# The weighted sum of gathered rows: from VectorE and TensorE half and half to TensorE alone

## What is computed

```python
def one(args):
    hh, ee, gg = args
    a = jnp.einsum("tkd,td->tk", peer_down[ee], hh, preferred_element_type=jnp.float32)
    act = (gg * jax.nn.gelu(a)).astype(hh.dtype)
    return jnp.einsum("tk,tkd->td", act, peer_up[ee])
```

## Time and profile before

| | us |
|---|---|
| median of 3 runs | 5476.44 |
| lowest, highest | 5467.74, 5490.61 |
| the profiled execution | 5502.99 |
| its span, first to last instruction | 5501.2 |
| TensorE matmuls busy, mean granted clock | 3615.6, 0.731 |
| VectorE busy | 2942.9 |
| GpSimd busy | 1960.8 |
| ScalarE busy | 816.3 |
| DMA moved | 1321.25 MB, of which 1073.87 by the indirect fetches |

### The profile page before, as it was taken

The page is one execution under the profiler, slowest core; times in us unless marked ns, Lnnn a source line. Parts: engine busy times, 40 slices in busy tenths (PEclk is TensorE's granted clock), DMA queues, the critical chain, the costliest instruction groups (busy, mean ns, idle before and its releaser), DMA issues.

```text
span 5501.2 us, 34464 instructions
## 1 busy us (share of the span) xinstructions
PE 3615.6 (66%) x9742; PEld 1773.4 (32%) x9742; DVE 2942.9 (53%) x5957; ACT 816.3 (15%) x1938; POOL 1960.8 (36%) x2058
## 2 busy tenths in 40 slices
PE   5778646887567667757575467751478885554566
PEld 1256413554212234315321111120256653221111
DVE  1211696547945766652476874540342223778766
ACT  1110112211101211111111110110131101111111
POOL 0000355435534656640254464430100000544665
PEclk8879757888688788865766567776688877666556
DMA  4235689988889999980487699870200003877999
GB/s 178 72 89 151 234 275 337 336 300 315 298 324 359 373 359 379 386 317 31 176 321 270 227 374 346 334 271 21 75 1 1 1 0 127 331 283 274 361 370 329
DMA packets 481787, 1321.25 MB, mean 240 GB/s; under 512 B 39884, under 2 KB 138444, under 8 KB 481088
## 3 DMA queue, kind: packets, MB, share of 16 engines
q0 software_dynamic: 294912, 1073.87, 52.4%
q1 hardware_dynamic: 179672, 219.30, 12.2%
q10 hardware_dynamic: 7016, 25.88, 1.3%
HBM read 1314.08 MB, written 1.17 MB: 239 GB/s over the span
## 4 chain that ended last, share of the span: by engine, by line
issue 22%; PE 20%; DMA 11%; POOL 8%; DVE 6%; SPq 2%; ACT 2%; another core or an unknown queue 1%; DVEq 0%; ACTq 0%; POOLq 0%
PE ps L1293 19%; POOL arena L2324 8%; DMA arena<-in_peer_up,arena 4%; DVE arena L637 2%; DMA arena<-in_peer_v,arena 2%; DVE arena L650 1%; DMA arena<-in_ada_w 1%; DMA arena<-in_peer_u,arena 1%; ACT arena L1878 1%; DVE ps L650 1%; SPq L2444 1%; DMA arena<-in_w_mod 1%; DMA arena<-mod_scratch 1%; PE ps L1299 1%
## 5 line engine op out<-in xcount | busy, mean ns | idle before, releaser
L1293 PE MATMUL ps<-arena 128*128 128x512 f32 (+12 forms) x9164 | 3501.1, 537 | 1555.9 <-DMA arena<-in_peer_up,arena 525.2
L1293 PEld LDWEIGHTS ps<-arena 128*128 128x128 f32 (+5 forms) x9164 | 1677.8, 216 | 3323.9 <-issue 2356.4
L650 DVE SCALAR_TENSOR_TENSOR arena<-arena,ps 128x1024 f32<-128x1024 f32 x1024 | 1245.2, 1216 | 394.2 <-DMA arena<-in_peer_down,arena 179.2
L2324 POOL DMA_INDIRECT arena<-in_peer_down,arena x768 | 723.4, 942 | 1715.1 <-DVE arena L654 965.9
L2324 POOL DMA_INDIRECT arena<-in_peer_up,arena x768 | 730.2, 951 | 476.7 <-issue 216.0
L650 DVE SCALAR_TENSOR_TENSOR ps<-arena,ps 128x512 f32<-128x512 f32 x1016 | 764.5, 753 | 190.9 <-DMA arena<-in_peer_up,arena 89.6
L1878 ACT ACTIVATE arena<-arena 128x128 f32<-128x128 f32 (+4 forms) x1251 | 448.3, 385 | 2586.2 <-issue 786.5
L2324 POOL DMA_INDIRECT arena<-in_peer_u,arena x256 | 240.5, 939 | 945.0 <-DVE arena L654 842.4
L637 DVE TENSOR_TENSOR arena<-ps,arena 128x512 f32<-128x512 f32 (+2 forms) x182 | 125.5, 690 | 636.5 <-PE ps L1293 598.9
L637 DVE TENSOR_TENSOR arena<-arena 128x16 f32<-128x16 f32 (+9 forms) x399 | 266.9, 669 | 222.4 <-DMA arena<-arena 148.1
L1878 ACT ACTIVATE arena<-ps 128x256 f32<-128x256 f32 (+3 forms) x341 | 172.9, 507 | 1274.8 <-PE ps L1293 896.8
(11 more groups left out here) (35 smaller groups left out, 563.4 us busy)
## 6 DMA issues: line engine op xcount, KB each, us to landing
arena<-in_w_mod SPq DMA_DIRECT2D x24, 2048.0 KB, 9.4
arena<-in_w_in SPq DMA_DIRECT2D x72, 512.0 KB, 5.5
arena<-in_w_pq SPq DMA_DIRECT2D x12, 2048.0 KB
arena<-in_ada_w SPq DMA_DIRECT2D x12, 2048.0 KB
arena<-in_w_in SPq DMA_DIRECT2D x8, 2048.0 KB, 20.0
arena<-in_w_out SPq DMA_DIRECT2D x8, 2048.0 KB, 7.7
arena<-mod_scratch ACTq DMA_DIRECT2D x30, 512.0 KB, 8.5
arena<-in_peer_down,arena POOLq DMA_INDIRECT x768
```

The source lines that it names most:

```text
L650: self.e.scalar_tensor_tensor(o, a, s, b, op0, op1, accum_out=accum).then_inc(*(inc or self.inc(self.S.vec)))
L1293: return self.e.matmul(o, l, r, start=start, stop=stop)
L2324: self.e.indirect_dma_start(out=o, out_offset=None, in_=table, in_offset=bass.IndirectOffsetOnAxis(ap=idx.bitcast(U32), axis=0)).then_inc( ...
```

## The change

For the up rows of a step TensorE makes two products with the same diagonal, columns 0 to 511 into `K.ap` and 512 to 1023 into `K.av`, and the second one increments `S.up_tensor`. VectorE's pass over the up rows, its waits for them and the semaphore `S.up_vector` are gone; POOL waits for `S.up_tensor` alone. In `fold`, `S.sum_read` is incremented by the third pass instead of the first.

```diff
@@ Vector.gather
                 n, k = divmod(u, NEXT)
                 c = base + u
-                w = K.AW[n % 2][:, k:k + 1]
-                self.wait_ge(S.up_in[c % NU], 16 * (c // NU + 1))
-                if k % GK == 0:
-                    self.wait_ge(*self.weighted)
-                src = K.us[c % NU][:, 512:1024]
-                if c:
-                    self.wait_ge(S.up_vector, c)
-                if k == 0:
-                    if c:
-                        self.wait_ge(S.tile_done, c // NEXT)
-                    self.ts(K.av, src, w, None, M, None, inc=self.inc(S.up_vector), free=True)
-                else:
-                    self.stt(K.av, src, w, K.av, M, AD, inc=self.inc(S.up_vector), free=True)
@@ Vector.fold
-        self.tt(K.tpb, K.ap, gr[:, 0:512], M, inc=self.inc(S.sum_read))
+        self.tt(K.tpb, K.ap, gr[:, 0:512], M)
         self.tt(self.X(t)[:, 0:512], self.X(t)[:, 0:512], K.tpb, AD)
-        self.tt(K.tpb, K.av, gr[:, 512:1024], M)
+        self.tt(K.tpb, K.av, gr[:, 512:1024], M, inc=self.inc(S.sum_read))
@@ Tensor.gather
-                self.mm(K.ap, K.dg[c % 4], K.us[c % NU][:, 0:512], k == 0, k == NEXT - 1).then_inc(*self.inc(S.up_tensor))
+                self.mm(K.ap, K.dg[c % 4], K.us[c % NU][:, 0:512], k == 0, k == NEXT - 1)
+                self.mm(K.av, K.dg[c % 4], K.us[c % NU][:, 512:1024], k == 0, k == NEXT - 1).then_inc(*self.inc(S.up_tensor))
@@ Pool.gather
                     self.wait_ge(S.up_tensor, c - NU + 1)
-                    self.wait_ge(S.up_vector, c - NU + 1)
```

More of the change, by code:

```diff
@@ L2591, in semaphores @@
     S.down_in, S.up_in = several("down_in", ND), several("up_in", NU)
-    S.diagonal, S.up_vector, S.up_tensor = one("diagonal"), one("up_vector"), one("up_tensor")
+    S.diagonal, S.up_tensor = one("diagonal"), one("up_tensor")
     S.sum_read, S.tile_done, S.keys_in = one("sum_read"), one("tile_done"), one("keys_in")
```

## The result

The changed kernel took 5503.95 us (median of ten runs, 5484.43 to 5520.59), the kernel before 5481.47 (ten, 5464.27 to 5509.59): ratio 1.0036, interval 1.0019 to 1.0053. Timed twice more, later, it gave 0.9997 (0.9978 to 1.0017) and 1.0002 (0.9980 to 1.0025). So the change costs between nothing and 0.4%, inside the half percent that I called no change. I had forecast 5550 and a slowdown as the likeliest case: the median moved by 22 us where I had 78.

What follows compares the result with a forecast made beforehand. Gather stretches alternate: clean ones paced by POOL's queue and DMA, others with VectorE or TensorE full. Terms -48 + 100 + 10 + 12 + 4 = +78 gave 5581 profiled, 5554 on the median, stated as 5550; range 5420 to 5680.

Steps and rivals of the forecast that it cites:

- Item 1: Gather stretches where VectorE is full, and phase starts: removing its passes saves 48 us, bounds -75 and -25.
- The two stretches: 620:820 and 1400:1540 us, VectorE full with top-k arithmetic woven in: 22 and 20 us gained.
- The step's cost: TensorE's time for a gather step with two products: 2.00 us at the full clock, 3.85 at the half one.
- Rival (c): Clean gather stretches: the clock is low for half of the 382 steps, +200 us on top, 5750; chance 0.08.
- The full stretch: 1040 to 1180 us, TensorE busy 134.7 of 140 us: the added products cost +25 us.
- rival (b): TensorE has room even where it looks full, so its woven stretches cost 0: sum -22, 5454; chance 0.08.
- item 2: Woven gather stretches with TensorE full or nearly: 0.90 us more a step, sum +100 us, bounds +50 and +150.
- 1560:1700: Woven stretch in us, 30 steps: 27 us of new work against 25 idle on TensorE, priced at +18.
- 3380:3520: Woven stretch in us, 23 steps: 21 us of new work against 25 idle, much before ada_w blocks; +15.
- 1800:2340: Woven stretch in us, 178 steps: TensorE 90% full beside a DMA share of 1.00; +20.
- Items 3 to 5: Costs in clean stretches (+10 us), at the ends of the phases (+12) and in the fold (+4).
- Rival (a): Woven stretches: TensorE's idle time takes the passes and VectorE's release had held the fetches; sum -32, 5444; chance 0.20.

Runs made afterwards that it cites:

- e2: Changed kernel without the second product, so nobody forms the upper half and the fold reads the lower half twice; 5308.74 us, ratio 0.9901 to the kernel before.
- e6: Changed kernel without the second product, but VectorE still waits in its queue for each up row; 5445.43 us against 5500.36, ratio 0.9898.
- e1: Kernel before with VectorE's pass kept and TensorE making the second product as well; 5423.97 us against 5360.32, ratio 1.0125.
- e3: Changed kernel in the first tile only (steps 0 to 127), the kernel before in the rest; 5352.59 us, ratio 0.9982.
- e7: Changed kernel with a third product a step in steps 256 to 511; 5597.15 us against 5500.36 of the kernel before, ratio 1.0172.
- e8: Changed kernel, but VectorE takes up steps 110 to 185 and from 256 on, its half sum copied at hand-over; 5458.42 us against 5488.45, ratio 0.9958.
- e11: e8 with VectorE's sum of up steps 110 to 185 kept in SBUF, without copy or wait; 5328.91 us against 5364.09 of the kernel before, ratio 0.9942.

## Why the forecast was wrong, step by step

**Item 1 was right in its sum.** -48 forecast; -53 (e2) and -56 (e6) measured. The two stretches hold less of it than I said, -17 and -17 us where I had -22 and -20; in e6's column the rest lies just around them, in the woven stretches and at the start of the second phase.

**The step's cost was right.** 503 records of the changed clean stretch cover 251.4 us: 2.00 us a step of four records. The pace stayed as it was (359.6 us for 360). Of the clock I had said 0.9, and it is 0.97. Rival (c) is out: it needed the low clock in half of these steps.

**The full stretch was right, and with it rival (b) wrong.** +33 for 1040:1180 and 1240:1380 together; the price of the table's stages 128 to 208 is 26.75 + 4.3 = 31 us. Before, weight loads covered 75% of 1040:1180. The Trainium skill ("Perfetto Trace Analysis", Identifying the Most-Contended Engine) judges TensorE's room by the share of peak arithmetic and by the busy share of the weight loads, not by matmul busy time. Here the weight loads cover 72% of the changed stretch (116.3 of 161.7 us) while TensorE has no idle time, and the stretch grew by nearly what was added. So the loads' share does not tell the room here, and the measurement decides: what told it was the idle time before the records (5.3 us before, and 25.7 us added made 21.7 longer).

**What failed is item 2's part for stretches that were not full**: 1560:1700 (+18), 3380:3520 (+15) and 1800:2340 (+20). 53 us were charged and about 2 are seen; e1 against e3 has -2 for the three. Two things were wrong in them. The first is a rule: I charged part of the new passes because the queues are in order and idle time "is waits for rows and banks". In 1800:2340 most of it was waits for rows (86 of 141 us) beside a DMA share of 1.00, and the new work shortened the waits and moved next to nothing; the price begins where the idle time ends (e7). That the transfers would have come no sooner is my reading of e6's windows. For 3380:3520, at a DMA share of 0.85, no run shows what held the stretch, only that the new records went into its waits for ada_w. The second is the clock, of which I counted too little. I had let it speed up the new passes, and in 1800:2340 the other 142 us of TensorE's work by 17. Measured, that other work went from 142.2 to 112.6 us (382.0 - 239.8, and 464.1 - 351.5), 30 less. In the other two stretches I had left this gain out; it is some 7 us in the first (81.7 to 74.9 on the modulation vectors) and 3 to 8 in the second (88.3 to 85.3 and 80.6 on ada_w's products).

**Items 3 to 5** (+26 together) were right as far as can be read: TensorE's price in all gather stages (mean of the two changed columns less e6, 752 to 768 left out) is 60 us, the ten stretches hold 33 of it, and 27 lie in the steps between (the short full one near 2850 us among them) and at the ends. How these divide over clock falls, phase ends and the fold was not measured, so that they came out is no proof of these terms.

**The sum.** Instead of -48 + 126 = +78 it is -53 to -56 for VectorE and +60 to +67 for TensorE: +4 to +14, and the three timings lie between -2 and +20. Since two numbers of about 60 cancel, no more than "within half a percent" was to be had from this sum, and a chance of 0.14 for it was too small.

**Rival (a)**, at -32, ended nearer than the forecast, in part by luck. Its condition, that TensorE's idle time takes new work freely, is nearly what the traces show. Its gain, that VectorE's release had held the fetches, did not come: POOL still waits 31.8 us for VectorE in 1785.8 to 2328.5, from a wait on the dot products that stays:

```profile
POOL arena L2311 <- PE ps L1280: 68.5, 49, 3.0
POOL arena L2311 <- DVE arena L650: 31.8, 23, 6.5
```

By number alone rival (b), at -22, came nearest, with a condition that is refuted: the full stretch paid.

**Slips in the prediction.** Rival (a) with the clean stretches at their lower bound is 5444 - 25 = 5419, not 5415. 239.8 us for 366 records is 1.31 us for each of 183 products, not of 178. Neither changes the forecast.

**Open.** e6 does less work than before and yet is 7 us longer in stage 272 to 336 (e8 6, the changed kernel 11 and 15); nothing was tried on it.

## What to carry to other kernels

Work that was moved here to an engine with idle time was nearly free until that idle time was used up, and cost nearly its whole length where there was none. Price a moved step by stretch, as max(0, new work - idle time), with the clock that the engine will then have for its other work too. With the measured busy times this gives 20.4 us for the full stretch (price 20.5), 46.7 for e7's third product (50.6), and 0 for the other six of rows 7, whose prices lie between -5 and +8. If the price falls in one stretch and the gain in another, divide the work by stretch, begin the division before the full stretch, and give each side a buffer of its own, so that neither queue waits at the hand-over. Read the times of stages between the same instructions of several executions; one profile on either side gave this change the other sign than the medians taken with it.

## What was not expected of the hardware

**The clock was higher with more work, and that paid for part of it.** TensorE's granted clock in the clean stretches went from 0.58 to 0.97 (levels 1.2 and 2.4 GHz) when one product a step became two: 251 records had taken 237.5 us, 503 take 251.4. The second product there cost 14 us of busy time in 126 steps, 0.11 us each, and no time at all.

**VectorE's passes with both operands in SBUF lengthened POOL's fetch instructions.** The groups by form from 960 to 1330 us, first of e11, then of e3, in which the same passes accumulate in PSUM:

```profile
L2346 POOL DMA_INDIRECT arena<-in_peer_down,arena x82 | 91.0, 1109 | 141.3 <-DVE arena L661 133.4 <-issue 7.9
L2346 POOL DMA_INDIRECT arena<-in_peer_up,arena x81 | 76.7, 947 | 60.9 <-PE ps L1310 40.5 <-issue 16.8 <-DVE arena L661 3.7
L661 DVE SCALAR_TENSOR_TENSOR arena<-arena 128x512 f32<-128x512 f32 x71 | 53.3, 751 | 0.0
```

```profile
L2331 POOL DMA_INDIRECT arena<-in_peer_down,arena x80 | 74.9, 936 | 151.3 <-DVE arena L651 145.2 <-issue 4.6 <-DVE ps L651 1.5
```

The passes take the same 0.751 us, but a down fetch takes 1109 ns of POOL on the mean instead of 936. It cost nothing that shows, since POOL had idle time before these fetches. e11's timeline has the single case:

```profile
1206.75 0.75 DVE L661 SCALAR_TENSOR_TENSOR arena<-arena 128x512 f32<-128x512 f32 x1
...
1207.11 1.20 POOL L2346 DMA_INDIRECT arena<-in_peer_down,arena  x1 [3.80 <-DVE arena L661]
...
1208.85 0.94 POOL L2346 DMA_INDIRECT arena<-in_peer_up,arena  x1 [0.54 <-PE ps L1310]
```

Over these 370 us, 58 down fetches overlap such a pass and take 1181 ns on the mean; the 24 others take 936, none over 1000. The usual case is a fetch that a dot product releases: it starts 0.35 us into the pass behind that dot product, with 0.395 us of it left, and takes 1.20 us. One with 0.22 left takes 1.03, with 0.48 left 1.29, with 0.61 left 1.42: what is left of the pass and 0.81 us. The Trainium skill ("SBUF — State Buffer", Who interferes with whom) has VectorE and GpSimd share a pair of ports that one of them holds for a whole instruction, among the cases an instruction of VectorE with two inputs in SBUF while the other reads SBUF. The longer down fetches agree with that. Most up fetches don't start inside such a pass. But eight start 0.06 us after one has begun and still take 0.94 us, which the rule does not explain.
